# One block for attention, decode and feed-forward, with the merge of attention's parts spread over the decode sequences

## What is computed

```python
h = rmsnorm(x, g_mix_pre) @ w_in                      # 1024 -> 2560 columns: A, B, C groups
for w, d in ((128, 1), (512, 4), (2048, 16)):         # A: 6 heads x 64, three strided windows
    o, lse = band_attention(aq, ak, av, bias, d, w // d)
o_a = sum_i softmax_i(lse_i) * o_i                    # merged per position by softmax denominators
o_b = band_attention(bq, bk, bv, bias, 1, 128)        # B: 6 query heads, 2 kv heads, window 128
o_b = o_b * sigmoid(lse_b - sink)
o_c = cb * conv3(cc * cx)                             # C: 256 channels
x = x + rmsnorm(concat(o_a, o_b, o_c) @ w_out, g_mix_post)
x = x + rmsnorm(relu(rmsnorm(x, g_mlp_pre) @ w_up) ** 2 @ w_down, g_mlp_post)
```

## Time and profile before

| | us |
|---|---|
| median of 3 runs | 2682.47 (2680.47 to 2683.25) |
| the profiled execution | 2681.24 |
| its span, first to last instruction | 2679.4 |
| PE busy | 2587.1 (97% of the span) |
| POOL busy | 1295.5 (48%) |
| ACT busy | 933.5 (35%) |
| DVE busy | 767.5 (29%) |

### The profile page before, as it was taken

One profiled execution on the slowest core, in us unless ns is written; L12 is line 12 of the kernel. 1 busy time (PEld: TensorE's weight loads), 2 busy tenths in 40 slices (PEclk: granted clock), 3 DMA queues, 4 the chain that ended last, 5 costly groups with the idle time before them and its releaser, 6 DMA issues.

```text
span 2679.4 us, 34851 instructions
## 1 busy us (share of the span) xinstructions
PE 2587.1 (97%) x13954; PEld 2238.6 (84%) x13954; DVE 767.5 (29%) x1658; ACT 933.5 (35%) x1586; POOL 1295.5 (48%) x832
## 2 busy tenths in 40 slices
PE   7999999979998959999999999999999999999998
PEld 6899999879996538788888888888888888998996
DVE  6431111156664223421112111133111224212113
ACT  4100110068775533432333333243333244332332
POOL 1200000046773356665555676465676466654553
PEclk9999999989999979999999999999999999999999
DMA  5211422199997954534443644354644243532432
GB/s 165 72 62 50 134 61 85 49 178 183 172 151 161 258 174 165 185 129 141 142 140 117 207 169 146 102 176 134 207 160 153 90 170 126 189 126 80 141 126 87
DMA packets 264102, 372.69 MB, mean 139 GB/s; under 512 B 78690, under 2 KB 199194, under 8 KB 259286
## 3 DMA queue, kind: packets, MB, share of 16 engines
q1 hardware_dynamic: 243696, 262.68, 34.9%
q10 hardware_dynamic: 14230, 89.10, 9.3%
q0 software_dynamic: 6016, 18.68, 2.4%
HBM read 322.38 MB, written 103.75 MB: 159 GB/s over the span
## 4 chain that ended last, share of the span: by engine, by line
PE 57%; POOL 2%; DVE 1%; ACT 1%; issue 1%; DMA 0%; ACTq 0%; SPq 0%; DVEq 0%; POOLq 0%
PE ml_y L1804 30%; PE ml_up L1762 8%; PE ml_up L1764 8%; PE ml_up L1763 8%; POOL ml_w_lo L1677 1%; PE ml_y L1799 1%; POOL em_hx L1673 1%; PE ml_y L1798 1%; DVE em_hx L2083 1%; PE ml_up L1747 1%; ACT ml_square L1902 0%; PE ml_up L1735 0%; POOL ml_a_lo L1686 0%; POOL em_y L1673 0%; DVE em_y L2083 0%
## 5 line engine op out<-in xcount | busy, mean ns | idle before, releaser
L1677 POOL TENSOR_TENSOR ml_w_lo<-em_raw,ml_w_hi 128x1024 fp32r<-128x1024 f32 x288 | 700.2, 2433 | 453.9 <-ACT ml_w_hi L1850 453.9
L1850 ACT CAST ml_w_hi<-em_raw 128x1024 fp32r<-128x1024 f32 x288 | 301.7, 1048 | 568.3 <-PE ml_y L1804 353.6
L1804 PE MATMUL ml_y<-ml_w_hi,ml_a_hi 128*128 128x512 f32 x1216 | 476.0, 391 | 1.4 <-POOL ml_w_lo L1677 1.4
L1804 PE MATMUL ml_y<-ml_w_hi,ml_a_lo 128*128 128x512 f32 x1216 | 473.4, 389 | 0.0
L1804 PE MATMUL ml_y<-ml_w_lo,ml_a_hi 128*128 128x512 f32 x1216 | 473.4, 389 | 0.0
L1762 PE MATMUL ml_up<-ml_h_hi,ml_w_hi 128*128 128x512 f32 (+1 forms) x1280 | 450.0, 352 | 1.7 <-POOL ml_w_lo L1677 1.7
L1764 PE MATMUL ml_up<-ml_h_hi,ml_w_lo 128*128 128x512 f32 (+1 forms) x1280 | 449.7, 351 | 0.0
L1763 PE MATMUL ml_up<-ml_h_lo,ml_w_hi 128*128 128x512 f32 (+1 forms) x1280 | 449.6, 351 | 0.0
L426 PE MATMUL pj_acc<-pj_h_hi,pj_w_hi 128*128 128x424 f32 (+1 forms) x800 | 289.3, 362 | 0.7 <-ACT pj_rstd_of L567 0.7
L427 PE MATMUL pj_acc<-pj_h_lo,pj_w_hi 128*128 128x424 f32 (+1 forms) x800 | 284.4, 355 | 0.0
L428 PE MATMUL pj_acc<-pj_h_hi,pj_w_lo 128*128 128x424 f32 (+1 forms) x800 | 284.1, 355 | 0.0
(11 more groups left out here) (260 smaller groups left out, 3367.0 us busy)
## 6 DMA issues: line engine op xcount, KB each, us to landing
em_raw<-in_w_up SPq DMA_DIRECT2D x64, 1024.0 KB, 5.3
em_raw<-in_w_down SPq DMA_DIRECT2D x64, 1024.0 KB, 5.2
out_o_a_k_s<-in_cache_a_k ACTq DMA_DIRECT2D x8, 3060.0 KB, 13.3
out_o_a_v_s<-in_cache_a_v ACTq DMA_DIRECT2D x8, 3060.0 KB, 12.1
em_raw<-scratch_pt SPq DMA_DIRECT2D x36, 512.0 KB, 7.7
em_raw<-in_w_out SPq DMA_DIRECT2D x16, 1024.0 KB, 5.1
scratch_pt<-pj_proj SPq DMA_DIRECT2D x10, 1056.0 KB, 4.0
pj_w<-in_w_in SPq DMA_DIRECT2D x20, 512.0 KB, 4.0
```

The lines of the kernel that those rows point to most:

```text
L1677: nc.gpsimd.tensor_tensor(split_of(w_lo, n), raw_of(n), f32(split_of(w_hi, n)), ALU.subtract).then_inc(w_lo_ready, 1)
L1804: last = pe.matmul(out, p[:, f, t0:t0 + m], w[:, b, :], start=(f == 0 and p is act_hi and w is hi), stop=(f == PF - 1 and p is act_lo))
L1850: nc.scalar.copy(split_of(w_hi, n), raw_of(n)).then_inc(w_hi_ready, 1)
```

## The change

`at` and `de` become phases within `em`, like `ml`, and `block()` hands all three the one block of `em`: the block's end, the clearing of semaphores and the barrier between `attend` and `decode`, and between `decode` and `out_and_mlp`, are gone, and `em`'s own at the end of the kernel stay. What the barriers had ordered is ordered by waits: POOL waits for the last matmul of `attend` before it clears decode's tiles, and SP's wait for the cache copies moves to the end of the kernel. The merge of tiles 0 to 5 is spread over the sequences by `merged_at`: the parts 0 and 1 are loaded behind the keys of sequence 2, one part each behind those of 3, 4, 5 and 6, and each later step of a tile follows one or more rounds of the loop later on its engine.

```diff
@@ Phase
     def block(self):
-        return self.ctx.enter_context(self.nc.Block())
+        if self.within is not None:
+            return self.within.block()
+        if self.whole is None:
+            self.whole = self.ctx.enter_context(self.nc.Block())
+        return self.whole
@@ attend
-    with Phase(nc, "at") as ph:
+    with Phase(nc, "at", early.phase) as ph:
...
-            sp.wait_ge(cache_out, 16 * DEC_B * 2)
+            early.caches_out = cache_out
...
+            early.weighed, early.o_copied, early.units = weighed, o_copied, NU
@@ out_and_mlp, the last wait of SP
+            sp.wait_ge(early.caches_out, 16 * DEC_B * 2)
@@ decode
-    with Phase(nc, "de") as ph:
+    with Phase(nc, "de", early.phase) as ph:
...
+        def merged_at(x):
+
+            return {0: (0, 1), 1: (2,), 2: (3,), 3: (4,), 4: (5,)}.get(x, ())
...
             for b in range(2, DEC_B):
                 load_keys(b)
-            for done, stores in zip(early.stored, early.stores):
-                sp.wait_ge(done, 16 * stores)
-            for t in range(MERGED_EARLY):
-                load_part(sp, d, early, t)
+                if b == 2:
+                    for done, stores in zip(early.stored, early.stores):
+                        sp.wait_ge(done, 16 * stores)
+                for t in merged_at(b - 2):
+                    load_part(sp, d, early, t)
...
         def _(pool):
+            pool.wait_ge(early.weighed, early.units)
             nc.gpsimd.memset(v_new[:], 0.0).then_inc(zeroed, 1)
...
-            for b in range(DEC_B):
-                load_values(b)
-            for t in range(MERGED_EARLY):
-                merge_difference(pool, nc, early, t)
-            for t in range(MERGED_EARLY):
-                merge_denominators(pool, nc, early, t)
-            for t in range(MERGED_EARLY):
-                merge_combine(pool, nc, early, t)
+            for b in range(DEC_B + 2):
+                if b < DEC_B:
+                    load_values(b)
+                for t in merged_at(b - 5):
+                    merge_combine(pool, nc, early, t)
+                for t in merged_at(b - 4):
+                    merge_denominators(pool, nc, early, t)
+                for t in merged_at(b - 3):
+                    merge_difference(pool, nc, early, t)
...
                 if c < DEC_B:
                     exp(c)
-            for t in range(MERGED_EARLY):
-                merge_shares(act, nc, early, t)
+                for t in merged_at(c - 3):
+                    merge_shares(act, nc, early, t)
...
                     lowest(c)
-            for t in range(MERGED_EARLY):
-                merge_lowest(dve, nc, early, t)
+                for t in merged_at(c - 4):
+                    merge_invert(dve, nc, early, t)
+                for t in merged_at(c - 2):
+                    merge_lowest(dve, nc, early, t)
             invert(DEC_B - 1)
-            for t in range(MERGED_EARLY):
-                merge_invert(dve, nc, early, t)
             mask(DEC_B - 1)
```

More of the change, by code:

```diff
@@ L67, in __init__ @@
     def __init__(self, nc, name, within=None):
-        self.nc, self.name, self.ctx, self.within = nc, name, ExitStack(), within
+        self.nc, self.name, self.ctx, self.within, self.whole = nc, name, ExitStack(), within, None
         self.semaphores = within.semaphores if within else []
```

## The result

The change makes the kernel faster, by less than forecast. Median of four runs each: 2668.68 us (2664.15 to 2669.88) against 2682.86 us (2680.47 to 2687.55), ratio 0.9942 with the 95% interval 0.9924 to 0.996. That is 14.2 us where 23.9 were forecast, and 2668.68 lies above the range of 2654 to 2665. The profiled pair differs by 2681.24 - 2669.05 = 12.2 us.

A forecast was written before the change was run, and what follows sets the result against it. PE, busy for 97% of the span, bounds the kernel, so only its standstills or low clock matter. 20.9 + 2.5 + 0.9 - 0.4 = 23.9 us off 2681.24 gives 2657.3, plus 1.23 for the median: 2658.5 us, range 2655 to 2663.

The forecast's parts named there:

- The second barrier (20.9 us): Between decode and feed-forward: without the barrier ACT goes straight on from its last store to its first split, 20.9 us less.
- The first barrier (2.5 us): Between attention and decode: DVE's wait ends and PE's first score comes sooner, 2.5 us won, between 0.4 and 3.5.
- The rule weighed against it: At the first barrier: two-port DVE copies and GpSimd instructions exclude each other; taken in full, the term shrinks to about 0.9 us.
- The keys of sequence 2 (0.9 us): In decode: these keys' loads start about 4 us sooner, so PE's wait for them goes, 0.9 us won (0 to 0.9).
- The parts' loads (term 0): In decode's rounds: at 335 GB/s a round with a part needs 14.0 us and nothing is late; 0, range to 3.6.
- The worst case in the prediction, 3.6 us: In decode: at 277 GB/s the six parts add 13.2 us of transfer, making keys 3.6 us late at worst.
- The first rival: In decode: parts ride at 277 GB/s, keys are late, up to 3.6 us lost and the 0.9; 2660 to 2663, chance 0.12.
- Merge work on POOL, DVE and ACT (0): In decode's rounds: the spread merge work fits beside PE's work, POOL's round 5 taking 13.3 of 14.92 us; 0 us.
- The second rival: In decode: POOL's round 5 with two combines runs too long, 1.9 us over; 2660 to 2662 us, chance 0.10.
- The entry's loads: At feed-forward's entry: weights and convolution columns land in time; the rival has them late, 5 us, 2664, chance 0.06.
- The clock (-0.4): Around both holes: low clock may end sooner (up to 2 us won) or reach first products (up to 1.7 lost); 0.4 lost.

The follow-up runs named there:

- spread_alone: The kernel before, both barriers kept, with only the parts' loads and merge work spread over the sequences; 2665.76 us, ratio 0.9934.
- after_again: The changed kernel, unaltered, run once more later beside other runs of the kernel before; 2662.36 us, ratio 0.9933.
- moved_filled: parts_moved with POOL's clearings behind the bias copies, two DVE inversions ahead of the last mask, and unread transposes in PE's holes; 2655.35 us, ratio 0.9903.
- parts_moved: The changed kernel with parts 0 to 3 loaded behind the keys of sequence 2, parts 4 and 5 behind those of sequence 7; 2665.6 us, ratio 0.9942.
- filled_long: The changed kernel with unread identity transposes on PE in its first hole, at decode's end and ahead of the first products; 2662.66 us, one execution.
- loads_spread: The changed kernel with its one block and spread part loads, but all merge work behind decode; 2677.47 us, ratio 0.9979.
- moved_queries_first: parts_moved with DVE's clearing and filling of the queries ahead of its three bias copies; 2663.47 us, ratio 0.9937.

## Why the prediction was right or wrong

**The second barrier (20.9 us): the size was right, the reason half wrong.** The entry gained 20.75 us by the table. But I had split the hole in "14.0 us of merge work and 7 us of closing" and put both down to the barrier's removal; the spread stood in the sum only as a condition. The runs show one cause: work of POOL that ended late, and POOL's drain of 7.0 us behind it. `spread_alone` closes ACT's part of the hole to 1.25 us with the barrier in place, and takes 18.9 of the 20.75 us. That the term came out is in part luck: the change held both edits.

**The first barrier (2.5 us): mis-sized.** Measured 0.8. The step that failed is "the memsets were hardly in DVE's way today, so I take a value near the upper half". They had been beside fills; now they stood beside copies, and these doubled. The rule weighed against it gave 0.9.

**The keys of sequence 2 (0.9 us).** The wait is gone as forecast, but a low clock from 857.5 to 860.9, behind PE's 2.0 us for ACT's copy, took it: by sequence 5, 0.3 us are left of 0.8 + 0.9. In `after_again`, with no low stretch there, 1.4 are left.

**The parts' loads (term 0): the failed step that cost most.** The prediction has "then a round needs 14.0 us and nothing is late", and the runs show waits of 2.9 and 5.5 us for keys, 4.4 and 8.3 us with what followed. Two things were wrong in it. I took 335 GB/s from a window that also held 1 MB loads of weights, and used it for rounds of keys; full rounds carried 268 to 302 here, and 262 over three rounds in `moved_filled`. And I counted 5.2 us of the pause and 4.4 behind it as free for the parts, though the change issues three parts ahead of the pause and three behind it, the last two among the keys of sequences 5 and 6. How much each of the two weighs is open, since the use of the pause differs between traces and doesn't go with the waits. The worst case in the prediction, 3.6 us, was exceeded even so: 2.9 us of waiting drew 1.5 us of low clock behind it, and `after_again` waited 5.5 us and lost 8.3 (from sequence 5 to 7 it took 38.1 us instead of 29.8). The first rival, at 0.12, was what happened, though its 2660 to 2663 us were too low for the first runs. The seven other kernels that left all six parts among the keys waited too, between 2.0 and 4.9 us.

**Merge work on POOL, DVE and ACT (0): right.** Round 5 combined two tiles, 13.3 us of POOL as forecast, and no wait of PE led to it. `parts_moved` kept this work for tiles 0 to 3 and had no wait in any round. The second rival is out.

**The entry's loads: right,** PE waited for none of them.

**The clock (-0.4): mis-sized, about 3.8 us.** 1.6 us at the first products (the prediction's bound of 1.7), 1.5 behind the late keys, 0.7 in the last weighing. `filled_long` and `moved_filled` show what it is worth: 4.7 and 5.2 us at decode's end and the entry, where the change left holes of 0.8 to 3.5 us.

In sum, against 23.9: first boundary -1.7, what lay between the first score and sequence 5 (the keys of sequence 2 among it) -1.4, late keys and their clock -4.4, decode's end -1.0, the entry with its clock, net of the forecast, -1.3, attention, the later wait and the tail -1.9. That leaves 12.2 us, the difference of the profiled pair. The last 1.9 are the 0.9 and 0.8 us named under the table and what attention differs by; why they are there is open, and they may be what executions differ by: in medians the gain is 14.2 and 18.3.

## What to carry to other kernels

Before you price a barrier, ask who comes to it last: what it costs is that engine's late work and its own closing (7.0 us of drain for POOL here), and moving this work away can win the same time with the barrier in place. Two edits that aim at one hole don't add. When loads are moved into a stretch whose DMA engines are full, take the rate from rounds of the same kind of transfer, and don't count a pause as free before a trace has shown it used. Price the clock with every hole, also one of 2 or 3 us: cheap transposes in PE's waits were worth more here than moving the loads and the clearings, once they covered nearly all of the wait. And take the trace of one kernel twice before you explain a microsecond with it: the wait for keys was 2.9 and 5.5 us in two traces of one program.

## What the runs showed of the hardware

- In the 17 traces, between attention and the first products, every hole of PE of 3.5 us or more has a stretch at 1.2 GHz in its last part or right behind it. Behind holes of 2.0 to 3.0 us the clock fell in some traces and not in others: behind 2.0 us in `loads_spread` (from 111.3 us, the wait ended at 110.4), but not behind 2.8 in `moved_filled` or 2.9 in `moved_queries_first`. Where transposes of the identity left less than 1 us of a hole, it stayed at 2.4 GHz. Filling 2.8 us of 6.9, or 1.7 of 3.7, left the low stretches behind them as long as in the change.
- In two traces of the same program PE waited 2.9 and 5.5 us for its keys. Windows of three rounds show 281 and 286 GB/s there, both with the DMA engines at 105%. Between kernels they show 262 (`moved_filled`) to 297 GB/s (`loads_spread`) at 104 and 105%.
- POOL's drain at a block's end took 7.0 us behind its last combine in two kernels, while those of the other engines at the same place took 1.2 us or less.
- DVE's copies of 48 partitions doubled beside POOL's clearings, but its own clearing of 1536 elements didn't (1.34 us with and without).
- A DVE instruction pair for low halves that reads `em_hx` took 3.93 instead of 1.28 us in `parts_moved`, when POOL's split of low weights had slid beside it. Three others, which read `ml_up`, a PSUM tile, took 1.89 us beside that split in the change, and 1.89 beside POOL's combines in `parts_moved`. The pair:

```profile
980.20 3.93 DVE L2018 TENSOR_TENSOR ml_h_lo<-em_hx,ml_h_hi 128x512 fp32r<-128x512 f32 x2
```
